# Memory keys and values of the sampled requests: DMAs issued by ScalarE instead of SyncE, in a fused decoder step

## The chip, the cores and the metric

The kernel runs as one program on one core of a Trainium2 chip. The metric is the device time of one execution in microseconds. The kernel before takes 2296.81 us, the median of 3 runs (2295.98 to 2301.11). One more execution was profiled; it took 2297.16 us, and its profile has a span of 2295.3 us.

## The reference, cut to what matters

One layer of a decoder trunk, all in float32, for two groups of tokens that share the weights: 256 prompt tokens and 8 requests of 8 tokens each.

```
h = rmsnorm(x);  q, k, v of two mixers = h @ w_in            # mixer A, 16 heads; mixer B, 16 query and 2 kv heads
x = x + concat(rmsnorm(mixerA), rmsnorm(mixerB)) @ w_out     # stage "out"
q = rmsnorm(x) @ w_cq                                        # stage "cq": 4 heads of 128
x = x + softmax(q @ mem_k.T / sqrt(128)) @ mem_v @ w_co      # 256 memory tokens; stage "co"
x = x + peer(rmsnorm(x) @ w_pq)                              # stage "pq": 8 heads choose 16 of 16384 experts each
y = rmsnorm(x)
```

For the prompt, the keys and values of the memory are computed from `mem_prompt`. For the sampled tokens they are inputs: `cache_mem_k` and `cache_mem_v`, 256 x 4 x 128 per request, 1 MB (2 x 512 KB) for each of the 8 requests. These are the transfers that the change touches.

## The kernel before

**Tiles.** The 320 tokens are cut in two groups, the first 128 prompt tokens ("first", 0) and the other 128 prompt tokens with the 64 sampled ones ("the rest", 1, 192 columns). The weights come in chunks of 1 MB (128 partitions x 2048 words); one chunk is the stationary operand of one output tile, 16 accumulated products of 128 x 128 by the group's tokens (for `co`, four tiles of 4 products). `TILES` lists the output tiles in the order in which TensorE (PE in the profile) works them off. The part that matters here is: `out` of the rest, tile 15; `pq` of the first, tiles 8 and 9; `cq` of the rest, tiles 0 to 3; `pq` of the first, 10 to 13, woven into the cross-attention of the rest; then `co` of the rest, tiles 0 to 15.

**The weight stream.** SyncE (SP) issues every chunk into a ring of 4 slots (`WR`). The loop over `STREAM` waits until TensorE has done with the chunk that is 4 places earlier (`s_used`), and then issues the DMA (L506). So at any time at most 4 chunks are landed or under way. In the kernel before, the same loop also issues the memory keys and values: `mem_keys(g)` (L479, one DMA of 2 MB for 4 requests, as 512 packets of 4 KB) and `mem_values(g, lo, hi)` (L483, one DMA of 512 KB for each request, 128 packets of 4 KB). A weight chunk is 128 packets of 8 KB. The two kinds share SyncE's one DMA queue (q1 in the profile).

**The cross-attention of the rest** is a software pipeline of six steps, v = 4 to 9, on three engines. v = 4 holds the sampled requests 0 to 3, v = 8 the requests 4 to 7, the others the heads of the prompt tokens. TensorE runs `scores_c(v)`, `turn_c(v)` (a transpose) and `values_c(v)`; VectorE (DVE) runs `max_c`, `norm_c` and `out_c`; ScalarE (ACT) runs `exp_c` and `turned_c`. `scores_c(4)` waits for the first keys (`s_km[0]`), `values_c(4)` for the first four values (`s_vm[0]`), `scores_c(8)` for the second keys (`s_km[1]`) and `values_c(8)` for the second four values (`s_vm[1]`). The second keys lie where the first did and so wait for `scores_c(4)`; two of the second values lie where two of the first did and wait for `values_c(4)`. Tile `pq` 10 stands behind `scores_c(4)` on TensorE, `pq` 11 behind `scores_c(5)`, and so on to `pq` 13. `co_tile(1, 0)` waits for the whole of the cross-attention (`s_cOev`).

**Expert rows.** In the same stretch VectorE works off one gathered expert row per step (`next_row`, L1268: a row of 2048 words for each of 128 tokens). GpSimd (POOL) issues these gathers (L561, 1 MB each, 128 packets of 8 KB, queue q0) into a ring of 3, each as soon as the row three places before is done with. VectorE waits for a row in its program order, so a late row holds back `out_c` and `out_requests` behind it.

**ScalarE in this stretch** squares the stream's tiles (`square`, L602), copies finished `pq` tiles (`keep_query`, L736), takes the root for the norm that `cq` of the rest needs (`root`, L619), and then runs `exp_c` (L683), `turned_c` (L691) and the copy of the requests' output (L778). VectorE's `group_inverse` (L897) and the 16 `group_norm` (L905) wait for that root, and the 16 products of `cq` tile 0 wait for the 16 norms one by one.

Of the kernel before, what the change touches and what calls it, by code (L numbers as in the profile page):

```python
# [112 lines left out]
POS = {chunk: C_OUT + i for i, chunk in enumerate(STREAM)}  # L113
FREED = {weights_of(tile): DONE[tile] for tile in TILES}
# [51 lines left out]
def build(nc, d):  # L166
    with ExitStack() as ctx:
# [96 lines left out]
        km = BIG[:, 0:4096]  # L264
        vm = [[BIG[:, at:at + 1024] for at in ats] for ats in ((4096, 13440, 22528, 23552), (6656, 14784, 4096, 13440))]
# [78 lines left out]
        s_used = sem("chunk_used")  # L344
# [20 lines left out]
        s_km = [sem("mem_keys_in0"), sem("mem_keys_in1")]  # L365
        s_vm = [sem("mem_values_in0"), sem("mem_values_in1")]
# [7 lines left out]
        s_cS, s_cmax, s_cexp, s_cnrm = sem("c_scores"), sem("c_max"), sem("c_exp"), sem("c_normed")  # L374
        s_cT, s_cTev, s_cO, s_cOev = sem("c_turned"), sem("c_turned_kept"), sem("c_out"), sem("c_kept")
        s_cpad = sem("c_pads")
        s_cV, s_cVev = sem("c_request_values"), sem("c_request_values_kept")
# [41 lines left out]
        V_FIRST, V_REQ, V_ALL = 0, (4, 8), 10  # L419
# [16 lines left out]
        def _(sp):  # L436
# [38 lines left out]
            sp.dma_start(d["kb_out"], HT[:, 4080:5104]).then_inc(s_attout, 16)  # L475
            sp.wait_ge(s_vb, 16)
            sp.dma_start(d["vb_out"], VB[:, :]).then_inc(s_attout, 16)
            def mem_keys(g):
                sp.dma_start(km.rearrange("p (n w) -> p n w", n=4), d["kmT"][4 * g:4 * g + 4].rearrange("n p w -> p n w")).then_inc(s_km[g], 16)  # L479

            def mem_values(g, lo, hi):
                for n in range(lo, hi):
                    sp.dma_start(vm[g][n], d["vm"][4 * g + n]).then_inc(s_vm[g], 16)  # L483

            for chunk in STREAM:
                pos, (stage, g, f) = POS[chunk], chunk
                before = pos - WR_N
                if before == POS["cq", 1, 0]:
                    sp.wait_ge(s_used, FREED["out", 1, 15])
                    mem_keys(0)  # L490
                    mem_values(0, 0, 4)
                    sp.wait_ge(s_sc, 3)
                    sp.wait_ge(s_idx, 3)
                    mem_values(1, 0, 2)
                if before == POS["pq", 0, 10]:
                    sp.wait_ge(s_cS, V_REQ[0] + 1)
                    mem_keys(1)
                if before == POS["pq", 0, 12]:
                    sp.wait_ge(s_cV, 1)
                    mem_values(1, 2, 4)  # L500
                if before < C_OUT:
                    sp.wait_ge(s_max, (4, 8, HEADS, HEADS)[pos - C_OUT])
                else:
                    sp.wait_ge(s_used, FREED[STREAM[before - C_OUT]])
                slot = slot_at(pos)
                sp.dma_start(WR[:, slot * D:(slot + 1) * D], d["wall"][IN_WALL[stage] + f]).then_inc(s_w[slot], 16)  # L506
# [63 lines left out]
        def _(act):  # L570
# [107 lines left out]
            def exp_c(v):  # L678
                act.wait_ge(s_cmax, v + 1)
                if v >= 2:  # L680
                    act.wait_ge(s_cT, v - 1)
                nb = v % 2
                nc.scalar.activation(probs_c[:, nb, :], score_out(v), ACT.Exp, bias=stat[:, 64 + nb:65 + nb], scale=MEM_SCALE, accum_out=stat[:, 66 + nb:67 + nb]).then_inc(s_cexp, 1)  # L683
# [47 lines left out]
            def keep_query(g, f):  # L731

                act.wait_ge(s_used, DONE["pq", g, f])
                src = tile_out("pq", g, f)
                if g == FIRST_TILE:
                    nc.scalar.activation(qp_first[f], src, ACT.Copy).then_inc(s_pev[0], 1)  # L736
                else:
                    nc.scalar.activation(qp[:, f, :], src[:, 0:P], ACT.Copy)
                    nc.scalar.activation(qs[:, f // 2 % (PH // 2), f % 2, f // PH, :], src[:, P:REST], ACT.Copy).then_inc(s_pev[1], 1)

            def keep_scores(c):
                t, h, n = GROUPS[c]
                act.wait_ge(s_sc, c + 1)
                nc.scalar.activation(sc[t][:, h * 256:(h + n) * 256], key_bank(c)[:, 0:256 * n], ACT.Copy).then_inc(s_scev, 1)

            def keep_rows(i, to, src):
                act.wait_ge(s_xt, i)
                nc.scalar.activation(to, src, ACT.Copy).then_inc(s_ht, 1)

            for f in range(3):  # L750
                keep_query(FIRST_TILE, f)
            keep_scores(0)
# [10 lines left out]
            for k in range(9, KT):  # L763
                square(THE_REST, CROSS, k)
                if k == 9:
                    keep_scores(2)
            keep_query(FIRST_TILE, 8)
            root(THE_REST, CROSS)
            keep_query(FIRST_TILE, 9)
            for it in range(7):  # L770
                if it < 6:
                    exp_c(4 + it)
                if it >= 1:
                    turned_c(4 + it - 1)
                if 4 + it - 2 in V_REQ:
                    r = V_REQ.index(4 + it - 2)
                    act.wait_ge(s_cV, r + 1)
                    nc.scalar.activation(o_req, bank[5], ACT.Copy).then_inc(s_cVev, 1)  # L778
                if it < 4:
                    keep_query(FIRST_TILE, 10 + it)  # L780
            keep_scores(3)
# [1338 lines left out]
```

## Time and profile before

| | |
|---|---|
| median of 3 runs | 2296.81 us |
| profiled execution | 2297.16 us, span 2295.3 us |
| TensorE busy | 2200.8 us (96%) |
| VectorE / ScalarE / GpSimd busy | 1182.0 / 295.8 / 377.6 us |
| DMA | 843.29 MB, mean 367 GB/s |
| of it SyncE's queue q1 / GpSimd's q0 / ScalarE's q10 | 485.30 / 354.58 / 2.11 MB |

The stretch of the change is 776 to 857 us of the span. It is read in four views: the chain of waits (the work that ended last), the timeline (every instruction in its order), the busy times by stretch with the granted clock of TensorE and what the DMA engines moved, and the DMA view, which counts packets by queue and gives the time from a DMA's issue to its landing. Times in the timeline are microseconds from the start of the span.

### The profile page before, as it was taken

The numbers are of one execution on the slowest core, as the hardware profiler recorded it, in microseconds if no ns is written. First come the engines' busy times: TensorE is split into PE (matmuls) and PEld (weight loads), VectorE is DVE, ScalarE is ACT, GpSimd is POOL, SyncE is SP. The second block draws the span as 40 slices with busy tenths as digits, with TensorE's granted clock in tenths as the row PEclk, the third lists the DMA queues.
The fourth block names the chain that finished last, engine by engine and source line by source line (L and its number), as shares of the span: only waits on it lengthen the run. The fifth ranks groups of instructions, "written<-read, shape, count | busy, mean of one in ns | idle before, by whom it ended". The sixth has DMA issues, their size and how long they took to land.

```text
span 2295.3 us, 35376 instructions
## 1 busy us (share of the span) xinstructions
PE 2200.8 (96%) x14282; PEld 2011.3 (88%) x14282; DVE 1182.0 (51%) x2115; ACT 295.8 (13%) x942; POOL 377.6 (16%) x414
## 2 busy tenths in 40 slices
PE   7999998799899979999999999999899999999998
PEld 5677776587689959999999999999899999999998
DVE  3200003844466658778785447788644444444402
ACT  2000001712220012011111012322100000000000
POOL 0100000023301021222222212222211111111100
PEclk9999999999999989999999999999999999999999
DMA  7999972289959898999999999999999999999964
GB/s 292 407 413 386 392 303 82 93 345 410 383 210 404 334 389 340 413 406 422 418 422 416 421 369 400 391 422 420 421 421 422 422 422 422 422 422 421 419 225 156
DMA packets 117792, 843.29 MB, mean 367 GB/s; under 512 B 14432, under 2 KB 16608, under 8 KB 30656
## 3 DMA queue, kind: packets, MB, share of 16 engines
q1 hardware_dynamic: 62752, 485.30, 52.5%
q0 software_dynamic: 54128, 354.58, 37.8%
q10 hardware_dynamic: 816, 2.11, 0.2%
q8 instruction: 63, 1.03, 0.2%
q14 instruction: 33, 0.27, 0.0%
HBM read 834.25 MB, written 74.78 MB: 396 GB/s over the span
## 4 chain that ended last, share of the span: by engine, by line
PE 75%; DMA 15%; DVE 6%; issue 2%; ACT 1%; POOL 1%; SPq 0%; DVEq 0%; POOLq 0%; ACTq 0%
PE low L1442 53%; PE big L1442 21%; DMA BIG<-expert_v,VB 6%; DMA BIG<-expert_u,VB 5%; DMA BIG<-kaT 2%; DMA BIG<-va 1%; DMA WR<-wall 1%; DVE BIG L1268 1%; ACT BIG L652 1%; DVE XT L1281 1%; DMA BIG<-memT 0%; DVE BIG L1279 0%; DVE CST L993 0%; POOL BIG L547 0%; DVE BIG L868 0%
## 5 line engine op out<-in xcount | busy, mean ns | idle before, releaser
L1442 PE MATMUL low<-HT,WR 128*128 128x176 f32 (+3 forms) x6360 | 1081.9, 332 | 9.1 <-DMA WR<-wall 7.2
L1442 PEld LDWEIGHTS low<-HT,WR 128*128 128x128 f32 x6360 | 986.3, 191 | 96.6 <-issue 8.1
L1442 PE MATMUL low<-BIG,WR 128*128 (+3 forms) x2616 | 433.8, 320 | 23.3 <-DMA WR<-wall 9.9
L1281 DVE SCALAR_TENSOR_TENSOR XT<-BIG,VB,XT 128x2048 f32<-128x2048 f32 x128 | 301.0, 2351 | 298.5 <-DMA BIG<-expert_v,VB 298.5
L1442 PE MATMUL big<-BIG,WR 128*128 (+3 forms) x2888 | 446.7, 310 | 0.8 <-DVE BIG L905 0.7
L1442 PEld LDWEIGHTS low<-BIG,WR 128*128 128x128 f32 x2616 | 410.6, 192 | 28.0 <-ACT CST L832 10.4
L1442 PEld LDWEIGHTS big<-BIG,WR 128*128 128x128 f32 x2888 | 417.8, 192 | 15.6 <-issue 15.5
L1268 DVE SCALAR_TENSOR_TENSOR BIG<-BIG 128x2048 f32<-128x2048 f32 x144 | 329.3, 2290 | 160.8 <-DMA BIG<-expert_u,VB 159.7
L561 POOL DMA_INDIRECT BIG<-expert_u,VB x144 | 168.1, 1168 | 682.5 <-DVE BIG L1268 603.5
L567 POOL DMA_INDIRECT BIG<-expert_v,VB x144 | 146.4, 1017 | 542.9 <-DVE XT L1281 473.3
L936 DVE TENSOR_SCALAR BIG<-low 128x320 f32 x32 | 15.8, 492 | 264.0 <-PE low L1442 264.0
L1442 PE MATMUL big<-BIG 128*32 128x256 f32 (+4 forms) x868 | 83.2, 383 | 10.7 <-ACT BIG L691 3.0
L1442 PEld LDWEIGHTS big<-BIG 128*32 128x32 f32 (+2 forms) x868 | 53.6, 144 | 32.6 <-DMA BIG<-va 6.3
L815 ACT ACTIVATE HT<-HT,VB 128x128 f32<-128x128 f32 x176 | 56.1, 390 | 179.5 <-DVE HT L1382 176.6
L841 ACT ACTIVATE HT<-XT 128x2048 f32<-128x2048 f32 x1 | 1.9, 1910 | 531.5 <-DVE XT L1281 531.5
L1382 DVE TENSOR_TENSOR HT<-CST,VB 128x512 f32<-128x512 f32 x88 | 56.6, 685 | 18.7 <-PE big L1442 18.7
L799 ACT ACTIVATE BIG<-low 128x176 f32 x80 | 25.4, 317 | 266.1 <-PE low L1442 251.6
L1442 PE MATMUL big<-HT 128*128 128x128 f32 x352 | 47.5, 278 | 3.8 <-ACT HT L815 3.8
L1425 DVE TENSOR_TENSOR XT<-XT,big 128x192 f32<-128x192 f32 x8 | 2.4, 351 | 92.2 <-PE big L1442 92.2
L1442 PEld LDWEIGHTS big<-HT 128*128 128x128 f32 x352 | 44.9, 191 | 4.9 <-issue 4.8
L533 POOL DMA_DIRECT2D HT<-kbT x1 | 0.5, 533 | 267.4 <-PE low L1442 267.4
L547 POOL DMA_DIRECT2D BIG<-kaT x56 | 29.7, 537 | 79.8 <-PE low L1442 79.8
(230 smaller groups left out, 1127.3 us busy)
## 6 DMA issues: line engine op xcount, KB each, us to landing
WR<-uT SPq DMA_DIRECT2D x128, 1024.0 KB
WR<-expert_v SPq DMA_DIRECT2D x128, 1024.0 KB
WR<-wall SPq DMA_DIRECT2D x122, 1024.0 KB
BIG<-va POOLq DMA_DIRECT2D x48, 512.0 KB, 13.5
BIG<-kaT POOLq DMA_DIRECT2D x64, 384.0 KB, 13.7
BIG<-kmT SPq DMA_DIRECT2D x2, 2048.0 KB, 17.4
BIG<-vm SPq DMA_DIRECT2D x8, 512.0 KB, 17.1
XT<-xT SPq DMA_DIRECT2D x1, 2560.0 KB, 21.7
```

Source lines behind the costliest of these rows:

```text
L547: pool.dma_start(kr[j][:, NEWK:SW], d["kaT"][n, j, :, FIRST:PAST]).then_inc(s_kr[j], 16)
L561: nc.gpsimd.indirect_dma_start(u_ring[n % URING], None, d["expert_u"], bass.IndirectOffsetOnAxis(eidx[:, n:n + 1], 0)).then_inc(s_ug[n % U ...
L567: nc.gpsimd.indirect_dma_start(v_ring[n % VRING], None, d["expert_v"], bass.IndirectOffsetOnAxis(eidx[:, v_slot(n):v_slot(n) + 1], 0)).the ...
L652: ins = nc.scalar.activation(parts[q][:, s], parts[q][:, s], ACT.Exp, bias=stat[:, c:c + 1], scale=1.0, accum_out=stat[:, c + 4:c + 5])
L799: nc.scalar.activation(C[:, bass.ds(i * (UB * DENSE) + r * DENSE, DENSE)], u_out[r], ACT.Gelu).then_inc(s_dev, 1)
L815: nc.scalar.activation(x, x, ACT.Copy, scale=turned[2][:, 4 * g + j:4 * g + j + 1]).then_inc(s_weighed, 1)
L936: nc.vector.tensor_scalar(QK[:, bass.ds(i * (4 * NT) + r * NT, NT)], bank[r % 2][:, 0:NT], 1.0, None, ALU.mult).then_inc(s_ev, 1)
L1268: nc.vector.scalar_tensor_tensor(out=u, in0=u, scalar=1.0, in1=h_tok if n < SLOTS else h_few, op0=ALU.mult, op1=ALU.mult, accum_out=dots[: ...
L1281: nc.vector.scalar_tensor_tensor(out=x_tok, in0=rows_of(row), scalar=weight, in1=x_tok, op0=ALU.mult, op1=ALU.add).then_inc(s_vsum, 1)
L1382: ins = nc.vector.tensor_tensor(hot[z][g % 2], iota.unsqueeze(1).broadcast_to([P, 4, NKEY]), turned[z][:, 4 * g:4 * g + 4].unsqueeze(2).br ...
L1425: nc.vector.tensor_tensor(x, x, v_all[k], ALU.add).then_inc(s_fx, 1)
L1442: return nc.tensor.matmul(out, lhsT, rhs, start=start, stop=stop, skip_group_check=True)
```

## The change

The DMAs for the memory keys and values of the sampled requests are taken out of SyncE's loop and put into ScalarE's program, with the same sources, destinations and semaphores. They now run in ScalarE's own DMA queue (q10). Sizes and packet shapes are as before. Their places: the first keys, the first four values and two of the second values stand after the last `square(THE_REST, CROSS, k)` and ahead of `keep_query(FIRST_TILE, 8)` and `root(THE_REST, CROSS)`; the second keys after `exp_c(4)`; the last two values after the copy of the first requests' output.

```diff
             for chunk in STREAM:
                 pos, (stage, g, f) = POS[chunk], chunk
                 before = pos - WR_N
-                if before == POS["cq", 1, 0]:
-                    sp.wait_ge(s_used, FREED["out", 1, 15])
-                    mem_keys(0)
-                    mem_values(0, 0, 4)
-                    sp.wait_ge(s_sc, 3)
-                    sp.wait_ge(s_idx, 3)
-                    mem_values(1, 0, 2)
-                if before == POS["pq", 0, 10]:
-                    sp.wait_ge(s_cS, V_REQ[0] + 1)
-                    mem_keys(1)
-                if before == POS["pq", 0, 12]:
-                    sp.wait_ge(s_cV, 1)
-                    mem_values(1, 2, 4)
...
+            def mem_keys(g):
+                act.dma_start(km.rearrange("p (n w) -> p n w", n=4), d["kmT"][4 * g:4 * g + 4].rearrange("n p w -> p n w")).then_inc(s_km[g], 16)
+
+            def mem_values(g, lo, hi):
+                for n in range(lo, hi):
+                    act.dma_start(vm[g][n], d["vm"][4 * g + n]).then_inc(s_vm[g], 16)
...
                 square(THE_REST, CROSS, k)
                 if k == 9:
                     keep_scores(2)
+            act.wait_ge(s_used, FREED["out", 1, 15])
+            mem_keys(0)
+            mem_values(0, 0, 4)
+            act.wait_ge(s_idx, 3)
+            mem_values(1, 0, 2)
             keep_query(FIRST_TILE, 8)
             root(THE_REST, CROSS)
             keep_query(FIRST_TILE, 9)
             for it in range(7):
                 if it < 6:
                     exp_c(4 + it)
+                if it == 0:
+                    act.wait_ge(s_cS, V_REQ[0] + 1)
+                    mem_keys(1)
                 if it >= 1:
                     turned_c(4 + it - 1)
                 if 4 + it - 2 in V_REQ:
                     r = V_REQ.index(4 + it - 2)
                     act.wait_ge(s_cV, r + 1)
                     nc.scalar.activation(o_req, bank[5], ACT.Copy).then_inc(s_cVev, 1)
+                    if r == 0:
+                        mem_values(1, 2, 4)
```

On SyncE, from the weight chunks of the rest's `out` to those of `pq` (BIG is the buffer of keys and values, WR the ring of weight chunks, `chunk_used` TensorE's count of finished chunks). The kernel before:

```order
L506 DMA WR<-wall 128x2048 [waits chunk_used] x50
L479 DMA BIG<-kmT 128x4x1024 [waits chunk_used]
L483 DMA BIG<-vm 128x1024 x4
L483 DMA BIG<-vm 128x1024 [waits experts_chosen,k_scores]
L483 DMA BIG<-vm 128x1024
L506 DMA WR<-wall 128x2048 [waits chunk_used] x4
L479 DMA BIG<-kmT 128x4x1024 [waits c_scores]
L506 DMA WR<-wall 128x2048 [waits chunk_used] x2
L483 DMA BIG<-vm 128x1024 [waits c_request_values]
L483 DMA BIG<-vm 128x1024
L506 DMA WR<-wall 128x2048 [waits chunk_used] x20
```

All ten of these DMAs leave SyncE; its 76 chunks follow one another with no other DMA between them, and the four behind the first block are those of `pq` 10 to 13.

On ScalarE, from the last squares to the copy of the requests' output, the kernel before:

```order
L602 ACTIVATE BIG<-XT 128x192 [waits stream_added_rest,group_squares_added_rest] x6
L736 ACTIVATE BIG<-low 128x128 [waits chunk_used]
L619 ACTIVATE BIG<-big,CST 128x192 [waits group_inv_rms_rest,group_square_sums_rest]
L736 ACTIVATE BIG<-low 128x128 [waits chunk_used]
L683 ACT_TABLE_LOAD [waits c_turned]
L683 ACTIVATE BIG,CST<-big,CST 128x256 [waits c_max]
L736 ACTIVATE BIG<-low 128x128 [waits chunk_used]
```

and the changed kernel, whose lines carry other numbers (L582 is the square, L716 the copy of a `pq` tile, L599 the root, L663 the exponential, L731 and L735 the keys and values):

```order
L582 ACTIVATE BIG<-XT 128x192 [waits stream_added_rest,group_squares_added_rest] x6
L731 DMA BIG<-kmT 128x4x1024 [waits chunk_used]
L735 DMA BIG<-vm 128x1024 x4
L735 DMA BIG<-vm 128x1024 [waits experts_chosen]
L735 DMA BIG<-vm 128x1024
L716 ACTIVATE BIG<-low 128x128 [waits chunk_used]
L599 ACTIVATE BIG<-big,CST 128x192 [waits group_inv_rms_rest,group_square_sums_rest]
L716 ACTIVATE BIG<-low 128x128 [waits chunk_used]
L663 ACT_TABLE_LOAD [waits c_turned]
L663 ACTIVATE BIG,CST<-big,CST 128x256 [waits c_max]
L731 DMA BIG<-kmT 128x4x1024 [waits c_scores]
L716 ACTIVATE BIG<-low 128x128 [waits chunk_used]
```

Seven DMAs now stand ahead of the root, and the second keys stand right behind the first exponential. The order on TensorE, VectorE and GpSimd is the same in both kernels.

## Rows read from the trace of the kernel before

**Rows 1.** Chain of waits, 740 to 960: start us, us, what

```profile
779.03 3.58 PE low L1442 x32
...
783.00 0.62 SPq L479
...
788.66 24.75 DMA WR<-wall
...
845.24 8.37 DMA BIG<-expert_u,VB
```

**Rows 2.** Timeline: start us, us, engine line op [idle before, releaser]

```profile
804.42 1.93 PE L1442 MATMUL big<-BIG 128*32 128x256 f32 x32 [1.01 <-DVE BIG L1105]
...
806.40 0.38 SPq L479 DMA_DIRECT2D BIG<-kmT  x1
...
813.54 6.18 PE L1442 MATMUL low<-HT,WR 128*128 128x128 f32 x32 [7.19 <-DMA WR<-wall]
...
820.21 3.74 PE L1442 MATMUL low<-HT,WR 128*128 128x128 f32 x32
...
835.67 1.93 PE L1442 MATMUL big<-BIG 128*32 128x256 f32 x32
...
851.14 2.29 DVE L1268 SCALAR_TENSOR_TENSOR BIG<-BIG 128x2048 f32<-128x2048 f32 x1 [3.80 <-DMA BIG<-expert_u,VB]
...
856.58 4.27 PE L1442 MATMUL low<-BIG,WR 128*128 128x192 f32 x16 [3.62 <-DVE BIG L1131]
```

**Rows 3.** Windows: us, busy PE, PEld, DVE, ACT, POOL, PEclk, DMA share, GB/s

```profile
777.00:784.00 7.00, 7.00 (x60) 7.00 (x59) 4.44 (x11) 2.04 (x4) 0.94 (x1) 1.00 0.99 385
791.00:847.00 56.00, 44.07 (x339) 36.65 (x337) 28.32 (x59) 6.57 (x22) 9.25 (x9) 0.90 1.02 419
```

**Rows 4.** Windows, a stretch of the dense stages behind

```profile
1050.00:1100.00 50.00, 50.00 (x338) 50.00 (x337) 40.32 (x87) 7.12 (x14) 11.72 (x10) 1.00 1.01 421
```

**Rows 5.** DMA view, second keys (806 to 807): count, KB each, us to landing

```profile
BIG<-kmT SPq DMA_DIRECT2D x1, 2048.0 KB, 22.0
```

**Rows 6.** DMA view, 776 to 857: queue, packets, MB, share of 16 engines

```profile
q1 hardware_dynamic: 3792, 19.92, 60.5%
q0 software_dynamic: 1666, 12.08, 36.8%
```

**Rows 7.** DMA view, issues in 776 to 838

```profile
WR<-wall SPq DMA_DIRECT2D x10, 1024.0 KB
...
BIG<-expert_u,VB POOLq DMA_INDIRECT x8
```

**Rows 8.** DMA view by queue, 796 to 799: rows against values

```profile
q0 software_dynamic: 100, 0.81, 65.0%
q1 hardware_dynamic: 112, 0.41, 34.1%
```

**Rows 9.** DMA view by queue, 80 to 82: weights against ScalarE's stores

```profile
q1 hardware_dynamic: 69, 0.63, 77.7%
q10 hardware_dynamic: 68, 0.28, 33.8%
```

**Rows 10.** Windows again, one stretch late in the cross-attention

```profile
842.00:852.00 10.00, 7.79 (x35) 4.47 (x35) 6.16 (x10) 1.71 (x5) 4.63 (x3) 0.52 0.98 394
```

**Rows 11.** ScalarE's own DMA issues: count, duration ns min/median/max, start

```profile
L635 ACTq DMA_DIRECT2D mk_out<-BIG x1: 393/393/393, 75.7 to 75.7; - x1
L636 ACTq DMA_DIRECT2D mv_out<-BIG x1: 1312/1312/1312, 76.1 to 76.1; - x1
```

**Rows 12.** Timeline, 774 to 790, ScalarE and VectorE around the root

```profile
775.62 0.36 ACT L602 ACTIVATE BIG<-XT 128x192 f32<-128x192 f32 x1 [3.10 <-DVE XT L913]
...
779.07 0.42 ACT L619 ACTIVATE BIG<-big,CST 128x192 f32<-128x192 f32 x1
...
780.91 5.36 DVE L905 SCALAR_TENSOR_TENSOR HT<-XT,CST,BIG 128x192 f32<-128x192 f32 x16
```

**Rows 13.** Who waited for whom, ScalarE, 760 to 900: us, times, longest

```profile
ACT BIG L683 <- DVE CST L1113: 30.5, 6, 22.8
```

More of the change, by code:

```diff
@@ L477, in _ @@
             sp.dma_start(d["vb_out"], VB[:, :]).then_inc(s_attout, 16)
[L478 to L483, printed above, removed]
             for chunk in STREAM:
```

## The prediction

> **What bounds the kernel now.** I read the chain of waits first. Between 783 and 814 us it does not run through TensorE. SyncE issues the memory keys at 783.00, six values behind them, and at 788.66 a weight chunk, whose DMA is on the chain for 24.75 us [rows 1]. Then the timeline: TensorE has ended `scores_c(4)` at 806.35 (804.42 + 1.93) and waits 7.19 us for that chunk, the one of `pq` tile 10; the tile takes 6.18 us, where the next one of the same shape takes 3.74 [rows 2]. So the queue's order costs 7.19 + 2.44 = 9.6 us at this place. In the windows the reader is to see why the chunk came late: the DMA engines move 385 GB/s in 777 to 784 and 419 GB/s from 791 to 847 [rows 3], a full pipe. The chunk stands in SyncE's queue behind 2.10 MB of keys and 3.15 MB of values, 12.5 us at 419 GB/s. A second wait is at the end of the stretch: VectorE waits 3.80 us for an expert row, and `co` tile 0 of the rest starts at 856.58 after that [rows 2]. From there on the order on every engine is as before, and TensorE is busy for all of the window from 1050 to 1100 [rows 4]; a shift at 856.58 should therefore reach the end of the span. The whole question is when `co` tile 0 starts.
>
> **The change, part by part.**
>
> *SyncE without the ten DMAs.* The chunk of `pq` 10 no longer stands behind 5.25 MB. It is issued when `cq` tile 0 ends, 0.8 us earlier at the most, and TensorE asks for it only at 806. Its wait of 7.19 us goes, and the slow 2.44 us with it. Taken alone: -9.6 us, so TensorE would be ready for `scores_c(8)`, which now starts at 835.67 [rows 2], at about 826 to 829.
>
> *The keys and values in a queue of their own.* What is late next is what `scores_c(8)` needs: the second keys. In the kernel before, they are issued at 806.40 and land 22.0 us later, at 828.4, ahead of need [rows 2, 5]. In the changed kernel they are issued at about 807 too, after `exp_c(4)`. But now they stand behind the first keys and six values in ScalarE's queue, and this queue has to share the engines with two others. How do queues share? Two places of the trace show it. From 796 to 799, rows of 8 KB (q0) and values of 4 KB (q1) pass 100 and 112 packets, 0.81 and 0.41 MB [rows 8]. From 80 to 82, weights of 8 KB (q1) and ScalarE's own stores of 4 KB (q10) pass 69 and 68 packets, 0.63 and 0.28 MB [rows 9]. The queues take turns packet by packet, and who has packets of 4 KB gets half the bytes. With all three busy ScalarE's queue gets one byte in five, about 84 of 419 GB/s.
>
> Now count packets until the second keys have landed. ScalarE's queue: 2 x 512 for keys and 6 x 128 for values, 1792. SyncE's: the chunks issued from 776 to 838 are ten [rows 7], with the one under way 11 x 128 = 1408. GpSimd's: eight rows [rows 7] and half of one, about 1090. In equal turns ScalarE's queue is the last to be done. So when the second keys land, nearly all else that has been issued has landed too, and bytes give the time. From 776 to 857, q1 moves 19.92 MB and q0 12.08 MB [rows 6]. Without the last two values (1.05 MB) and the rows whose gathers are issued only after `scores_c(8)` (12.08 less the 8.5 rows, 3.15 MB), 27.8 MB are left. At 419 GB/s that is 66.4 us; from 776, with under a microsecond for the time until the pipe is full, the second keys land at about 843. Lower bound: the last two chunks and the last row, issued late, are still under way (3.15 MB, 7.5 us); the keys land at 835.5. Upper bound: one byte in five to the end, 7.34 MB at 84 GB/s from 777.5, which is 865. I take 843, since the other queues run dry before the upper bound and their packets are fewer. `scores_c(8)` then starts 843 - 835.67 = 7.3 us later than before, instead of 7 earlier.
>
> The first values pass the same count: keys and four values (1024 packets, 4.19 MB), seven chunks (7.3 MB) and 5.5 rows (5.8 MB) are 17.3 MB, 41 us, so 817 to 818; `values_c(4)` stands behind `pq` 11, which ends at 824 now [rows 2], and could run at 815 then. That uses up part of TensorE's lead and costs nothing against before. The last two values come right behind the keys, 1.05 MB or 2.5 us, at 845.5; `values_c(8)` stands 8 us behind `scores_c(8)`, so they are not waited for.
>
> *Behind `scores_c(8)`.* Four things follow. The rows of steps 7 and 8 are gathered when the pipe is nearly empty, since SyncE's four slots are full by then. The chain has 8.37 us for such a row with others under way [rows 1]; 2.5 us of it is the sharing at most, and I take half, -1.2 us. The wait for the keys, some 14 us, drops TensorE's clock as the wait of 7.19 us did, and the first 5 us behind it run at half speed. But in the kernel before, the clock here is also down, 0.52 from 842 to 852 [rows 10], so of up to 2.4 us I take 0.9. The sum at `co` tile 0: 7.3 - 1.2 + 0.9 = +7.0 us.
>
> *ScalarE's own time.* Seven issues now stand between the last square (ends 775.98) and the root (779.07) [rows 12]. On SyncE the seven took 5.66 us, 783.00 to 788.66 [rows 1]; ScalarE's own two took 0.39 and 1.31 us [rows 11]. So 2.9 us (7 x 0.39 and the gaps) to 9.5 us, and the root comes 0 to 6.5 us late; by SyncE's figure it comes 2.9 us late. The reciprocal and the 16 norms follow; the first norm is there at 781.25 (780.91 and a sixteenth of 5.36) [rows 12], and `cq` tile 0 starts when `pq` 9 ends, at 782.62 [rows 1], so there are 1.4 us to spare: TensorE loses 0 to 5 us, likely 1.5. This is hidden: TensorE's lead at `scores_c(8)` is 9.6 us and it waits there. If the keys were not late, it would be the price of the change. The three later issues (about 1.2 us) lie in time in which ScalarE waits, 30.5 us in six exponentials [rows 12, 13]: nothing.
>
> Sum: 2297.16 + 7.0 = 2304.2 us in the profiled execution's terms; that execution was 0.35 us above the median of the runs shown, so 2303.8.
>
> **The rivals.**
>
> *The turn of the queues gives the keys enough (faster).* If the second keys land by 829, both gains stay: -9.6, and 1.5 back for ScalarE's issues. But the pipe stays full, and the rows at the end set a floor: 32 MB from 776 at 419 GB/s are through at 852.4, against 857. So about -5 us, 2292. For it: the chunk's wait is real and goes. Against it: the packet counts of [rows 8, 9].
>
> *The pipe decides, whatever the order (no change).* The same 32 MB pass before `co` tile 0 in both kernels. If the last two chunks let the keys go first, these land at 835.5 to 837 and `scores_c(8)` starts where it did: 2296 to 2298, say 2297. For it: the lower bound above, and 419 GB/s all along. Against it: the ten chunks have fewer packets than ScalarE's queue. Two statements of the Trainium skill bear on this. "DMA: Bandwidth & Descriptors", section "Issuing engines are not separate DMA queues", says that issuing from several engines saves only the sequencer's issue time, since all run on the same engines; by it the change brings the 0.8 us of the issue, which is hidden. The bandwidth in [rows 3, 9] agrees with the shared engines, not with order being without effect. The same page of the Trainium skill, section "Queues, rings and completion order", says that an engine drains a whole packet of some 9 to 17 descriptors from one queue before it turns to the next. By it the keys, 32 pieces on each engine, would pass in larger turns than the weights' 8, and the end is this rival's. The equal counts in [rows 8, 9] come from transfers of 8 pieces and cannot exclude it for the keys.
>
> *Both keys and first values late (slower still).* If ScalarE's queue gets less than its turn, `values_c(4)` slips past 824 too and `scores_c(8)` to 850: +13 us, 2310.
>
> **How the numbers follow.** The forecast has 0.62, the first rival 0.10, the second 0.22, the last 0.06. What a measurement can tell from no change is 0.2%, 4.6 us here. Around its value of +7.0 the forecast is spread by some 3 us, so a tenth of it falls within 0.2%: slower 0.56 + 0.06 = 0.62; same 0.06 + 0.22 and 0.02 of the first rival, whose -5 us lies near the bound, 0.30; faster 0.08. The forecast's own range is 2300 to 2308. The given one reaches down to take in the second rival and stops short of the first: 2295 to 2309.
>
> **What would show it.** Right: no wait for WR before `pq` 10, a wait for a keys DMA of some 14 us before `scores_c(8)`, the second keys 30 us or more from issue to landing, q10 at about half of q1's packets' bytes, `co` tile 0 at 862 to 865. Wrong, if the second keys land within 25 us of their issue, if a window between 776 and 843 shows q10 with more bytes than q1 while both have packets, or if the shift at `co` tile 0 does not come back at the end of the span.

## The result, and the profile after

The changed kernel takes 2307.91 us (median of 15 executions, 2301.69 to 2315.12), the kernel before 2299.49 us on the same chip (15 executions, 2294.95 to 2301.32). The ratio is 1.0040, with a 95% interval of 1.0032 to 1.0048: slower by 9.2 us (7.4 to 11.0). The forecast was 2303.8 us, in a range of 2295 to 2309, as a rise of 7.0 us over 2296.81; 2.7 us of the 4.1 that 2307.91 lies above it are the kernel before, which takes 2299.49 here. The profiled execution has a span of 2306.8 us, against 2295.3 before.

Both profiles reach the stretch of the change at slightly different times: the last product of `out` tile 15 ends at 775.13 before and at 776.30 after. So 1.2 us of every shift below is older than the change.

The chain of waits of the changed kernel, 770 to 885 (start us, us, what), answers to [rows 1]:

```profile
779.43 42.60 DMA BIG<-vm
...
822.16 3.64 PE big L1439 x16
...
835.65 11.23 issue
846.88 3.67 PE big L1439 x32
...
858.14 7.35 DMA BIG<-expert_u,VB
...
868.46 5.49 PE low L1439 x16
```

The weight chunk is gone from the chain. In its place stand two others: the first values, which TensorE waits for until 822, and 11 us in which TensorE waits before the 32 products at 846.88, `scores_c(8)`. The profile names no releaser there ("issue"); the DMA rows below do. TensorE's timeline, the rows that answer to [rows 2]:

```profile
807.48 3.84 PE L1439 MATMUL low<-HT,WR 128*128 128x128 f32 x32
...
822.16 3.64 PE L1439 MATMUL big<-BIG 128*32 128x512 f32 x16 [6.19 <-DMA BIG<-vm]
...
846.88 3.63 PE L1439 MATMUL big<-BIG 128*32 128x256 f32 x32 [11.23 <-issue]
...
868.46 1.97 PE L1439 MATMUL low<-BIG,WR 128*128 128x192 f32 x5 [7.12 <-DVE BIG L1128]
```

`pq` 10 starts at 807.48 with no wait and takes 3.84 us. `scores_c(8)` starts at 846.88 instead of 835.67, and `co` tile 0 at 868.46 instead of 856.58. Less the 1.2 us, that is 10.0 and 10.7 us later. From there the spans run on for 1438.3 us (after) and 1438.7 us (before): the shift reaches the end whole.

The DMA view shows whose data was late. The second keys, issued at 808.26 (the last figure is the time to landing, so 846.8), answer to [rows 5]:

```profile
BIG<-kmT ACTq DMA_DIRECT2D x1, 2048.0 KB, 38.5
```

38.5 us, where it was 22.0. The queues from 800 to 823 (packets, MB, share of 16 engines):

```profile
q1 hardware_dynamic: 528, 3.89, 40.7%
q0 software_dynamic: 527, 3.79, 39.7%
q10 hardware_dynamic: 529, 1.94, 21.1%
```

All three queues have work, and in 23 us they pass 528, 527 and 529 packets. ScalarE's, of 4 KB, carry a fifth of the bytes. From 777 to 847, until the second keys have landed:

```profile
q1 hardware_dynamic: 1584, 11.54, 40.0%
q0 software_dynamic: 1239, 8.97, 30.8%
q10 hardware_dynamic: 2179, 8.29, 29.7%
...
WR<-wall SPq DMA_DIRECT2D x10, 1024.0 KB, 13.0
```

28.8 MB pass first, at a mean of 412 GB/s. 11.5 MB of them are weights, eleven chunks; ten are issued in this window. The windows (us, busy PE, PEld, DVE, ACT, POOL, granted clock, DMA share, GB/s):

```profile
800.00:822.00 22.00, 14.97 (x131) 13.43 (x129) 12.87 (x29) 2.53 (x9) 3.75 (x4) 0.95 1.02 419
...
835.60:847.00 11.40, 0.17 (x5) 0.15 (x8) 0.00 (x0) 0.28 (x1) 0.00 (x0) 0.70 0.99 404
847.00:857.00 10.00, 7.06 (x58) 3.52 (x61) 6.32 (x15) 1.68 (x6) 0.94 (x1) 0.83 0.09 23
```

From 835.6 to 847 the five engines stand almost still while the pipe (the 16 DMA engines together) is full; then the pipe is nearly empty (23 GB/s) for 10 us, because SyncE's four slots are full and GpSimd issues its next gather only at 854.75. In the kernel before, the pipe was full until about 850 and TensorE worked beside it.

ScalarE's timeline, which answers to [rows 12]:

```profile
776.81 0.41 ACTq L731 DMA_DIRECT2D BIG<-kmT  x1
777.25 3.69 ACTq L735 DMA_DIRECT2D BIG<-vm  x6
...
781.16 0.41 ACT L599 ACTIVATE BIG<-big,CST 128x192 f32<-128x192 f32 x1
```

The seven issues take 4.1 us, and the root is 0.9 us later than before (781.16 against 779.07 and the 1.2 us).

### The profile page after: what moved, and what is told of

It reads as the page before. It is cut to its first block, busy times and chain, and to the rows that moved or that the text cites. A ratio compares the mean times of both kernels' runs of the same rounds, so it can differ in the third digit from the quotient of the medians.

```text
span 2306.8 us, 35375 instructions
## 1 busy us (share of the span) xinstructions
PE 2201.1 (95%) x14282; PEld 2008.6 (87%) x14282; DVE 1182.1 (51%) x2115; ACT 295.7 (13%) x942; POOL 373.6 (16%) x414
## 4 chain that ended last, share of the span: by engine, by line
PE 74%; DMA 17%; DVE 5%; issue 2%; ACT 1%; POOL 1%; ACTq 0%; SPq 0%; DVEq 0%; POOLq 0%
PE low L1439 53%; PE big L1439 20%; DMA BIG<-expert_v,VB 6%; DMA BIG<-kaT 4%; DMA BIG<-expert_u,VB 3%; DMA BIG<-vm 2%; DVE BIG L1265 1%; DMA WR<-expert_v 1%; ACT BIG L632 1%; DMA BIG<-va 1%; POOL BIG L527 1%; DMA WR<-wall 1%; DVE XT L1278 1%; DMA BIG<-memT 0%; DVE CST L990 0%
## 5 line engine op out<-in xcount | busy, mean ns | idle before, releaser
L1439 PE MATMUL big<-BIG 128*32 128x256 f32 (+4 forms) x868 | 83.0, 386 | 29.1 <-issue 11.2
L1422 DVE TENSOR_TENSOR XT<-XT,big 128x192 f32<-128x192 f32 x8 | 2.4, 350 | 92.2 <-PE big L1439 92.2
```

What stands on the lines that cost most here:

```text
L1422: nc.vector.tensor_tensor(x, x, v_all[k], ALU.add).then_inc(s_fx, 1)
L1439: return nc.tensor.matmul(out, lhsT, rhs, start=start, stop=stop, skip_group_check=True)
```

## Experiments

Each was run beside the kernel before on its chip. One table first. The profiles start the stretch at different times, so the distance from the end of `out` tile 15 to the start of `scores_c(8)` and of `co` tile 0, from each timeline, is the better measure of place.

| kernel | to `scores_c(8)`, us | to `co` 0, us | ratio to before (95%) |
|---|---|---|---|
| before | 60.5 | 81.5 | 1 |
| changed | 70.6 | 92.2 | 1.0040 (1.0032 to 1.0048) |
| e1, second block back on SyncE | 59.7 | 80.6 | 0.9991 (0.9983 to 1.0000) |
| e2, first block back on SyncE | 61.9 | 81.2 | 0.9999 (0.9989 to 1.0009) |
| e3, changed, keys in 16 KB packets | 58.5 | 80.3 | 0.9995 (0.9985 to 1.0005) |
| e4, changed, keys in 2 KB packets | 72.8 | 94.6 | 1.0061 (1.0046 to 1.0076) |
| e5 and e12, changed, issues behind the root | 66.4; 66.3 | 87.3; 86.3 | 1.0014 (1.0004 to 1.0024); one execution |
| e6, SyncE, in order of need | 60.4 | 81.1 | 0.9998 (0.9990 to 1.0007) |
| e7, e6 with 16 KB keys | 59.6 | 80.6 | 0.9999 (0.9990 to 1.0008) |
| e9 and e13, split, 16 KB keys | 54.0; 55.7 | 78.5; 80.7 | 0.9994 (0.9982 to 1.0007); 0.9983 (0.9973 to 0.9993) |
| e10, e6 without 2.1 MB | 58.2 | 80.5 | 0.9989 (0.9980 to 0.9998) |
| e11, e6 without 4.2 MB | 51.4 | 71.5 | 0.9958 (0.9944 to 0.9971) |

**e1, the second block back on SyncE.** The second keys and the last two values are issued by SyncE at their old places; the first block stays on ScalarE.

```diff
+                if before == POS["pq", 0, 10]:
+                    sp.wait_ge(s_cS, V_REQ[0] + 1)
+                    mem_keys(1)
+                if before == POS["pq", 0, 12]:
+                    sp.wait_ge(s_cV, 1)
+                    mem_values(1, 2, 4)
```

> Half of the change: first keys, first values and two of the second values on ScalarE's queue; the second keys and the last two values back in SyncE's queue at their old places. Theory of turns (queues pass packets one for one, so 4 KB packets beside 8 KB packets lag, and the second keys were late because they stood behind 5.2 MB in the lagging queue): the wait of 7 us for the chunk of pq 10 stays away, values_c(4) still waits some 6 us for the first values (landing at 820 to 823), but the second keys land at 827 to 832, before scores_c(8) is ready at about 836. co tile 0 starts at 853 to 857; time 2 us faster to equal to before, 8 to 11 us faster than the changed kernel. Rival, ScalarE's time (seven issues ahead of the root): they are all still there, so as slow as the changed kernel. Rival, a third queue makes the engines' pipe less efficient: most of the loss stays.

Measured: 2297.59 us, 2.1 us below the kernel before, with an interval that ends at none. TensorE's timeline:

```profile
813.21 3.74 PE L1447 MATMUL low<-HT,WR 128*128 128x128 f32 x32
824.37 3.64 PE L1447 MATMUL big<-BIG 128*32 128x512 f32 x16 [6.99 <-DMA BIG<-vm]
...
837.45 1.93 PE L1447 MATMUL big<-BIG 128*32 128x256 f32 x32
```

No wait for a chunk and none at `scores_c(8)`: the second keys land at 835.4, 2 us before they are needed, if 3 us later than expected. The 7.0 us that the chunk used to cost is now the wait of `values_c(4)` for the first values. The whole slowdown is gone with the second block's place alone.

**e2, the first block back on SyncE.** The reverse: only the second keys and the last values are issued by ScalarE.

```diff
+                if before == POS["cq", 1, 0]:
+                    sp.wait_ge(s_used, FREED["out", 1, 15])
+                    mem_keys(0)
+                    mem_values(0, 0, 4)
+                    sp.wait_ge(s_sc, 3)
+                    sp.wait_ge(s_idx, 3)
+                    mem_values(1, 0, 2)
```

> The other half: the first block (first keys, first values, two of the second values) back in SyncE's queue, only the second keys and the last two values on ScalarE's queue. Theory of turns: the wait of 7 us for the chunk of pq 10 is back; the second keys, issued at about 807 and alone in their queue, need 512 turns of 30 ns (one other queue) to 49 ns (two), so they land at 824 to 833, before they are needed at 835.7. No wait for keys. Time as before, within 2 us. So each half alone costs nothing and only the two together cost 8 us or more. Rival, ScalarE's time: also as before, since no issue stands ahead of the root. Rival, queue efficiency: between the two, 2 to 5 us slower than before.

Measured: 2299.64 us, as before.

```profile
815.86 5.95 PE L1448 MATMUL low<-HT,WR 128*128 128x128 f32 x32 [8.79 <-DMA WR<-wall]
...
837.75 1.93 PE L1448 MATMUL big<-BIG 128*32 128x256 f32 x32
```

The chunk's wait is back (8.79 us), and the second keys are in time. So neither half of the change costs anything by itself. The loss needs both: the second keys in a queue in which the first block still stands.

**e3 and e4, the size of the keys' packets.** Both are the changed kernel. In e3 a key transfer is 128 packets of 16 KB, in e4 1024 of 2 KB. The input array is laid out in memory to fit; the bytes and their place on the chip are the same.

```diff
-                act.dma_start(km.rearrange("p (n w) -> p n w", n=4), d["kmT"][4 * g:4 * g + 4].rearrange("n p w -> p n w")).then_inc(s_km[g], 16)
+                act.dma_start(km, d["kmT"][g]).then_inc(s_km[g], 16)        # e3; e4 cuts the same rows in halves, n=8
```

> The changed kernel with the keys laid out in memory so that each partition's 4096 words are one run (a change of layout of the input alone, same bytes, same DMAs, same places): the keys' packets become larger, 16 KB or at least 8 KB in place of 4 KB. Theory of turns: the keys take 2 to 4 times the bytes per turn. First keys land by 790, first values before 816 (a wait of at most 2 us at values_c(4)), second keys before 830, no wait of 11 us at scores_c(8). co tile 0 starts at 850 to 855; 8 to 14 us faster than the changed kernel and 2 to 6 us faster than before. Rivals, ScalarE's time and queue efficiency and sheer bytes: no change against the changed kernel (within 2 us).

> The opposite dose: the changed kernel with the keys' packets of 2 KB in place of 4 KB (1024 packets per DMA of keys; same bytes, a change of layout of the input alone). Theory of turns: the first keys need 1024 turns of about 45 ns, landing at 815 to 825, so scores_c(4) itself waits 10 to 18 us; everything in ScalarE's queue comes later. 15 to 30 us slower than before, 7 to 20 us slower than the changed kernel. Rivals, ScalarE's time, queue efficiency, sheer bytes: as the changed kernel, within 3 us.

Measured: e3 2297.89 us, as before and 10 us below the changed kernel; e4 2312.47 us. The queues of e3 from 822 to 830, then those of e4 from 838 to 845:

```profile
q10 hardware_dynamic: 116, 1.78, 52.6%
q0 software_dynamic: 114, 0.80, 24.0%
q1 hardware_dynamic: 113, 0.79, 23.9%
```

```profile
q0 software_dynamic: 177, 1.28, 44.1%
q1 hardware_dynamic: 178, 1.23, 42.4%
q10 hardware_dynamic: 173, 0.44, 16.0%
```

The counts are equal again, and the bytes follow the size of the packet: 53% for 16 KB against 8 KB, 15% (0.44 of 2.95 MB) for 2 KB. That is the mechanism of the forecast, turned up and down. Two things went otherwise than expected. The first is that e3 is not faster than the kernel before, although no wait of its `pq` tiles for a chunk is left. TensorE in e3:

```profile
834.18 3.64 PE L1439 MATMUL big<-BIG 128*32 128x256 f32 x32 [5.97 <-issue]
...
846.68 3.64 PE L1439 MATMUL big<-BIG 128*32 128x512 f32 x16 [4.43 <-issue]
```

The second keys, issued at 809.13, land 25.0 us later, at 834.1: `scores_c(8)` is 2.1 us nearer than before, but TensorE has stood 6.0 us for them, and 4.4 us more at `values_c(8)` for the last values, whose last part lands at 846.6. The other is e4. It loses 14.0 us (10.6 to 17.5), where 15 to 30 were expected, and not in the way that was expected. `scores_c(4)` does not wait for its keys, for they land at 797.8 and not at 815 to 825: at times the other two queues had little or nothing to pass meanwhile (from 783 to 785, q10 passes 255 packets, q1 31 and q0 none). And part of its loss arises on ScalarE:

```profile
779.23 12.23 ACTq L735 DMA_DIRECT2D BIG<-vm  x6
...
791.68 0.42 ACT L599 ACTIVATE BIG<-big,CST 128x192 f32<-128x192 f32 x1
```

Behind a key transfer of 1024 packets the six issues take 12.2 us instead of 3.7. The root comes 9.5 us later from the end of `out` than before, TensorE then waits 8.3 us for the first norm, and `scores_c(4)` stands 39.7 us from the end of `out` instead of 29.3. So e4's size says little of the queues alone; its packet counts do.

**e5 and e12, the seven issues behind the root.** The same kernel twice.

```diff
+            keep_query(FIRST_TILE, 8)
+            root(THE_REST, CROSS)
             act.wait_ge(s_used, FREED["out", 1, 15])
             mem_keys(0)
...
-            keep_query(FIRST_TILE, 8)
-            root(THE_REST, CROSS)
```

> The changed kernel with the block of seven DMAs moved behind the root (keep_query 8 and root first, then the keys and values). Theory of turns: the root is no longer 1 to 1.5 us late, but the DMAs start 2.5 to 3 us later; what bounds is the landing of the second keys, and that is the sum of bytes ahead of it, so the waits at values_c(4) and scores_c(8) stay (together 15 to 20 us), and the time is that of the changed kernel within 2 us. Rival, ScalarE's time ahead of the root is what costs: 3 us or more faster than the changed kernel, near before.

> The same kernel as e5_after_root, for a second profile. That run had a median of 2301.4 us with executions from 2296.2 to 2309.5, and its profiled execution was the slowest (span 2307.4: first values 13.3 us late for values_c(4), the first expert rows and chunks ahead of them). Theory (the turns of the three queues fall differently from one execution to the next, since ScalarE's queue starts later there): a typical execution has the same kind of wait, for the first values, but shorter, 4 to 9 us, and a span of 2297 to 2303. Rival (the profiled execution was typical and the timed ones differ in nothing that the order of the queues decides): the wait is 13 us again and the span 2306 to 2308.

Measured: e5 2301.37 us, 3.2 us (0.9 to 5.5) above the kernel before, so about 6 us better than the change. That was not expected: the root had been found to cost nothing. e12, one execution, took 2303.51 us. TensorE in e5, then in e12:

```profile
832.83 3.64 PE L1439 MATMUL big<-BIG 128*32 128x512 f32 x16 [13.32 <-DMA BIG<-vm]
...
846.29 1.93 PE L1439 MATMUL big<-BIG 128*32 128x256 f32 x32
```

```profile
830.54 3.64 PE L1439 MATMUL big<-BIG 128*32 128x512 f32 x16 [13.35 <-DMA BIG<-vm]
...
843.85 1.93 PE L1439 MATMUL big<-BIG 128*32 128x256 f32 x32
```

Both profiles show the same waits, 13.3 us before `values_c(4)` and none before `scores_c(8)`; the theory that the turns fall differently each time falls, though e12's span of 2301.5 us is in its range. What differs is the start of the stretch: `out` tile 15 ends at 779.86 in e5's profile and at 777.55 in e12's. Net of it, `co` tile 0 is 5.8 and 4.8 us later than before. And the cause is not the root: `scores_c(4)` stands 29.3 us from the end of `out` in e5, as in the changed kernel. In the changed kernel TensorE waits 6.2 and 11.2 us; here it waits once, 13.3 us, and earlier. While it stands, no chunk is used up and no expert row worked off, so fewer are issued. From 784 to 843, when e5's second keys have landed:

```profile
q1 hardware_dynamic: 1216, 8.78, 35.9%
q10 hardware_dynamic: 2162, 8.24, 34.8%
q0 software_dynamic: 1008, 7.34, 30.6%
```

This window starts 4.1 us behind the end of `out`. Counted from the end of `out` to the landing of the second keys in both kernels, 26.0 MB pass in e5 and 29.1 MB in the changed kernel: 9.5 MB of chunks instead of 11.5, two fewer, and 8.1 MB of rows instead of 9.2, one fewer. The keys wait for less, and land at 842.8 (issue at 811.8 and 31.0 us). That this is why the second wait went is argued from the counts; no run separates it. Why the first values land 7 us later from the end of `out` than in the changed kernel, where their block is issued only 3.4 us later, stays open.

**e6 and e7, all on SyncE, in the order of need.** The values of the first block go one to three places further down in SyncE's loop, between the chunks; in e7 the keys have 16 KB packets too.

```diff
                 if before == POS["cq", 1, 0]:
                     sp.wait_ge(s_used, FREED["out", 1, 15])
                     mem_keys(0)
-                    mem_values(0, 0, 4)
+                if before == POS["cq", 1, 1]:
+                    mem_values(0, 0, 2)
+                if before == POS["cq", 1, 2]:
+                    mem_values(0, 2, 4)
+                if before == POS["cq", 1, 3]:
                     sp.wait_ge(s_sc, 3)
```

> All ten DMAs in SyncE's queue as before the change, but in the order of need: first keys, chunk of pq 10, two values, chunk of pq 11, two values, chunk of pq 12, two of the second values, chunk of pq 13, second keys. One queue, so nothing takes turns but the rows. Theory of turns: no wait of 7 us for pq 10, no wait for values or keys of more than 3 us at one place (the pipe is full, 32 MB by 852); co tile 0 starts at 850 to 854, so 3 to 6 us faster than before. Rival, sheer bytes decide (32 MB at 419 GB/s are needed before co tile 0 whatever the order): within 2 us of before.

> As the kernel with SyncE's order of need, and the keys in packets of 16 KB. In SyncE's queue the keys then take twice the bytes of the rows per turn, while a row waits longer for its turns. Theory of turns: the keys land 1 to 2 us earlier, rows that pass beside them 1 to 2 us later; time within 2 us of the kernel with the order of need alone. It tells whether large packets help by themselves (then 3 us or more faster) or only by their turn against another queue.

Measured: 2298.07 and 2298.54 us, as before. The expected gain of e6 is missing, and large packets alone, in SyncE's queue, bring nothing, as expected of e7. The timeline of e6:

```profile
828.82 6.08 PE L1446 MATMUL low<-HT,WR 128*128 128x128 f32 x32 [5.07 <-DMA WR<-wall]
...
836.70 1.93 PE L1446 MATMUL big<-BIG 128*32 128x256 f32 x32 [1.80 <-issue]
...
857.36 4.58 PE L1446 MATMUL low<-BIG,WR 128*128 128x192 f32 x16 [6.36 <-DVE BIG L1135]
```

The waits have changed place and size (the chunk of a later `pq` tile 5.1 us, the keys 1.8 us, and 6.4 us before `co` tile 0 for VectorE, which works off the last row), and `co` tile 0 stands where it stood.

**e9 and e13, the first block on ScalarE and the second on SyncE, keys in 16 KB packets.** The same kernel twice: e1 with e3's packets.

> First block on ScalarE's queue, second keys and last two values in SyncE's queue, all keys in packets of 16 KB. Theory of turns: the first keys are through by 790 and no longer hold up the first values, which land at about 812 instead of 822; the 7 us wait at values_c(4) goes. The second keys, in SyncE's queue and in wide packets, land by 832, and scores_c(8), ready at about 828 to 830, waits 3 us at most. co tile 0 starts at 851 to 855: 2 to 5 us faster than before and than the kernel with 4 KB keys in the same places. Rival, sheer bytes: as that kernel, 2297 to 2299.

> The same kernel as e9_split_wide (first keys and six values on ScalarE's queue, the second keys and last values on SyncE's in their old place, keys in packets of 16 KB), which measured 0.9994 of the kernel before with an interval of 0.9982 to 1.0007, too wide to tell. Theory (it starts co tile 0 some 3 us earlier, since no chunk waits and the second keys have their turn; the floor of the bytes allows about 4): ratio 0.9985 to 0.9995. Rival (nothing is gained but the order): 0.9995 to 1.0005.

Measured: 2295.97 us (0.9994, which tells nothing from no change), and when run again 2296.69 us, 0.9983 (0.9973 to 0.9993), 3.9 us below the kernel before. TensorE's timeline in e13:

```profile
832.72 3.18 PE L1447 MATMUL big<-BIG 128*32 128x256 f32 x32 [3.00 <-issue]
...
844.92 3.64 PE L1447 MATMUL big<-BIG 128*32 128x512 f32 x16 [4.59 <-issue]
...
857.73 5.25 PE L1447 MATMUL low<-BIG,WR 128*128 128x192 f32 x16 [5.59 <-DVE BIG L1136]
```

`scores_c(8)` is 4.8 us nearer than before, `co` tile 0 only 0.8 us (3.0 in e9): from the one to the other it takes 25 us, where it takes 20.9 before. The two waits above are for the second keys (they land at 832.6) and for the last values (their last part lands at 844.8). But the chain of waits there does not run through the values. It runs through an expert row, which takes 11.22 us (10.90 in e9) where it takes 8.37 before:

```profile
843.54 11.22 DMA BIG<-expert_u,VB
```

It is gathered while the pipe is still full (from 843 to 850, q1 moves 1.69 MB beside the rows' 1.29), and VectorE waits for a row twice, 4.3 and 2.5 us. It is the best version found, if a gain of one to four us is taken as one.

**e10 and e11, bytes left out.** e10 is e6 without the values of requests 4 to 7 (2.1 MB): `values_c(8)` multiplies with the values of requests 0 and 1. e11 leaves out the second keys too (4.2 MB in all): `scores_c(8)` multiplies with the first keys. The engines' work is the same.

```diff
-                    mem_values(1, 0, 2)
...
-                    mem_keys(1)          # e11 only
...
-                    mem_values(1, 2, 4)
```

> As the run e6_order_of_need (everything on SyncE, each transfer in the place where it is needed), and the values of requests 4 to 7 (four DMAs, 2.1 MB) are left out: values_c(8) multiplies with the values of requests 0 and 1 again, so the work on the engines is the same. Theory (the bytes bound this stretch: 32 MB must pass between 776 and 851 at about 419 GB/s before the last expert rows, whatever their order): everything behind the first block comes 2.1 MB / 419 GB/s = 5.0 us earlier. pq tile 10 starts at 826 instead of 828.8, co tile 0 of the rest at 852 to 853 instead of 857.4, the time is 2292.5 to 2294 against 2298 for the kernel before (ratio about 0.998). Rival (fixed latencies of the rows' gathers and TensorE's own work bound it): co tile 0 within 1 us of 857, time 2297 to 2298.5.

> As e10_no_second_values, and the second keys (one DMA of 2.1 MB) are left out too: scores_c(8) multiplies with the keys of requests 0 to 3. 4.2 MB less in all. Theory (bytes bound): up to 10 us earlier at co tile 0 than in e6_order_of_need. But TensorE's own work from 783 on with no wait ends at about 847, and the wait of pq tile 10 (826 instead of 820) stays for 2 to 3 us, so co tile 0 comes at 848 to 851 and the time is 2289 to 2292 (ratio 0.996 to 0.9975). Rival (fixed latencies): no more than 1 us below the kernel before, 2297 to 2298.5.

Measured: e10 2298.63 us, 2.5 us (0.5 to 4.6) below the kernel before, about half of what was expected, though the interval reaches the lower expected values; e11 2290.98 us, 9.7 us (6.7 to 12.9) below. TensorE in e10, then in e11:

```profile
837.41 3.64 PE L1439 MATMUL big<-BIG 128*32 128x256 f32 x32 [7.22 <-issue]
...
859.67 4.42 PE L1439 MATMUL low<-BIG,WR 128*128 128x192 f32 x16 [6.58 <-DVE BIG L1128]
```

```profile
829.56 1.93 PE L1436 MATMUL big<-BIG 128*32 128x256 f32 x32
...
849.62 5.49 PE L1436 MATMUL low<-BIG,WR 128*128 128x192 f32 x16 [7.29 <-DVE BIG L1125]
```

In e10 no chunk waits any more, but the second keys do: `scores_c(8)` is 2.2 us nearer than in e6, and then takes 3.64 us instead of 1.93 behind its wait of 7.2 us (granted clock 0.50 from 837.4 to 841). The queues of e10 from 826 to 832:

```profile
q0 software_dynamic: 185, 1.26, 51.2%
q1 hardware_dynamic: 299, 1.22, 50.5%
```

Half of the bytes are expert rows. So, as far as one window shows, bytes taken from one queue come back to the one that waits only in part. With the keys' own 2.1 MB gone as well (e11) there is nothing to wait for, and 9.9 us go at `co` tile 0. Of the twelve kernels e11 is furthest below the one before. It also has neither the second keys nor the last values to wait for, so it does not tell fewer bytes from fewer waits.

## Why the prediction was right, point by point

**The chunk's wait goes: right.** `pq` 10 starts at 807.48, when `scores_c(4)`'s products end (805.61 + 1.93), and takes 3.84 us. The 7.19 and 2.44 us were both given back at that place.

**Equal turns, packet by packet: right.** 528, 527 and 529 packets in one stretch of 23 us, and the same at 16 and at 2 KB. e3 shows that it is the cause and not a companion: with larger packets alone, in the same queue at the same place, the loss is gone. From 800 to 823, q10 passes values, 8 pieces on each engine, since the first keys landed at 797.0. Two other places show it for keys: in the changed kernel from 791 to 793, with the first keys under way (32 pieces on each engine), q1 and q10 pass 68 packets each; in e4 from 838 to 845, with the second keys (64 pieces), the three queues pass 177, 178 and 173. The rule of the Trainium skill in "DMA: Bandwidth & Descriptors", section "Queues, rings and completion order", that an engine drains a whole packet of some 9 to 17 descriptors before it turns to the next queue, would have given the keys larger turns than the chunks' 8; these equal counts do not agree with that. Nor does the time agree with what the same page of the Trainium skill says in section "Issuing engines are not separate DMA queues", that only the issue time is saved: the engines are shared, as it says, but with the same bytes the kernel became 9.2 us slower.

**Second keys at 843: right, 2.6 us short.** They landed at 846.8, or 845.6 less the 1.2 us. The term that was mis-sized is the bytes that pass before: 27.8 MB forecast, 28.8 MB passed. The forecast left the last two values (1.05 MB) out, as coming behind the keys. But by 847 q10 had moved 8.29 of its 8.39 MB (2 x 2.10 of keys and 8 x 0.52 of values): they pass beside the keys' last packets. The landing events of the keys' 16 parts lie between 840.5 and 846.8, so the 16 engines are not in step with one another. 1 MB is 2.4 us at 419 GB/s. The rate was a little high, too: over the whole stretch it is 412 GB/s, worth another 1.1 us, and a start of the stretch that was taken 0.8 us late gives most of that back.

**The lower bound (835.5) was real.** It stood for two chunks and a row that do not get ahead. In e5 two chunks and a row fewer pass, and the second keys land 63 us from the end of `out` instead of 70.5. What seems to decide is whether TensorE's earlier wait holds chunks and rows back, which the forecast did not name.

**First values at 817 to 818: 3 us short.** They landed at 822.0 (820.8 net). TensorE waited 6.2 us for them, which cost nothing against before (`values_c(4)` ran at about 824 there): as forecast, the lead was used up.

**Behind `scores_c(8)`: the terms off, the sum near.** Forecast -1.2 from the rows and +0.9 from the clock. The chain's row takes 7.35 us instead of 8.37: -1.0. `scores_c(8)` takes 3.63 us instead of 1.93, +1.7: the granted clock is 0.52 from 846.9 to 850.5 (1.2 GHz is 0.5, 2.4 GHz is 1.0), behind a wait of 11.2 us, and it was 1.00 in these products before (835.6 to 837.6). The forecast took 0.9 because the clock before is down from 842 to 852 [rows 10], but that is behind `scores_c(8)`. Sum +0.7 instead of -0.3; with 10.0 for the keys, 10.7 at `co` tile 0, where 7.0 was forecast, and 9.2 (7.4 to 11.0) measured at the end. Two of the signs named in advance were missed for the same reasons: `co` tile 0 starts at 867.3 net, behind the 862 to 865, and TensorE's wait for the keys is 11.2 us and not some 14, because 6.2 us of its lead had gone to the first values.

**ScalarE's own time: right.** 0.9 us late at the root, inside 0 to 6.5 and under the 2.9 taken, and hidden: `scores_c(4)` stands 29.3 us from the end of `out` in both kernels. That it can grow, e4 shows (12.2 us for six issues).

**The rivals.** "The pipe decides" did not hold for this change, but it comes near for all that is better: every order in which the second keys land by 837, e1, e2, e3, e6, e7 and e9, ends within about 2 us of the kernel before, whether a chunk waits in it or not, and only e11, with fewer bytes and fewer waits, goes well below. Outside that band, with all the bytes, is only e13, the kernel of e9 run again, 3.9 us below. The reason, as far as it is shown: from `scores_c(8)` to `co` tile 0 it takes 19.3 to 22.3 us in every kernel but e9 and e13, since the last rows are gathered only behind it; and in e9 and e13, where `scores_c(8)` comes earliest with all the bytes, the row on the chain takes 11 us instead of 8.4. The forecast's 9.6 us of gain at `pq` 10 found no way to the end in any kernel here. "The turn gives the keys enough" is false at 4 KB and nearly true at 16 KB (e3, keys at 834.1), but even there the -5 us that it was priced at did not come: -1.1 us (-3.4 to +1.1). "Both late" came in a mild form: the first values were late too, by less than cost anything.

**The chances.** With a spread of 3 us around +7.0, if it is a standard deviation, about a fifth of the forecast falls under the 4.6 us, not a tenth. That moves some 0.07 from slower to same; the order of the outcomes stays.

**Open.** Which part of e10's missing 2 to 3 us is the clock and which the rows is argued from one profile. That the start of the stretch wanders by up to 5.8 us between profiles (774.1 to 779.9 at the end of `out`) was seen and not explained.

## What to carry to other kernels

Before a transfer is moved to a queue of its own, count packets, not bytes: beside two busy queues it got a third of the turns here, and its share of the bytes was set by its packet size, so a late and urgent transfer must not stand there behind 3 MB of early ones in small packets. Removing a wait in a stretch with a full pipe brought little or nothing here; ask which bytes the end of the stretch needs, and whether the last of them comes earlier. Judge each half of such a change alone as well: here both halves were free, and together they cost 9 us.

## What the runs showed of the hardware that was not expected

- Three queues with work passed 528, 527 and 529 packets in 23 us, and 116, 114 and 113 when one had packets of 16 KB: turns by count at every size tried (2, 4, 8 and 16 KB), at 419 to 424 GB/s in sum, and with 64 pieces on each engine (e4) as with 8.
- ScalarE's six value issues took 3.59 to 4.10 us behind a key transfer of 512 packets (changed, e1, e5, e12), 3.54 to 4.25 us behind one of 128 (e3, e9, e13), and 12.23 us behind one of 1024 (e4, one profile).
- A stop of TensorE can go with a faster transfer: in e5, behind an earlier wait of 13.3 us, two chunks and a row (3.1 MB) fewer passed before the second keys had landed, and the next wait of 11.2 us was gone.
